# Attention loop of a hybrid encoder: one stretch of attention work per step instead of three breaks in the projections

## The reference, cut to what matters

```python
proj = h @ w_in                       # (1024, 1024) x (1024, 10240), in fp32
qkv = proj[..., :N_DIL * 3 * A_WIDTH].reshape(bsz, s, N_DIL, 3, A_HEADS, A_HEAD_DIM)
for g, (window, dil) in enumerate(DILATION_PAIRS):      # three groups
    o, l = _dilated_group(qkv[:, :, g, 0], qkv[:, :, g, 1], qkv[:, :, g, 2], window, dil, slopes)
# in a group: scores = q.k/8 + alibi; p = exp(scores - m); o = p @ v / z; lse = m + log(z)
wts = softmax(stack(lses))            # merges the three groups per head
y = (merged * silu(gate)) @ w_out
```

## Time and profile before

| | us |
|---|---|
| median of three runs | 2309.37 |
| the profiled execution | 2316.02 |
| its span, first to last instruction | 2314.2 |
| TensorE busy | 2149.2 (93%) |
| VectorE / ScalarE / GpSimd busy | 1085.6 / 939.5 / 829.3 |
| mean granted clock of TensorE | 0.977 of full speed |

### The profile page before, as it was taken

The page is one execution under the profiler, slowest core; times in us unless marked ns, Lnnn a source line. Parts: engine busy times, 40 slices in busy tenths (PEclk is TensorE's granted clock), DMA queues, the critical chain, the costliest instruction groups (busy, mean ns, idle before and its releaser), DMA issues. The chain is left out here.

```text
span 2314.2 us, 32869 instructions
## 1 busy us (share of the span) xinstructions
PE 2149.2 (93%) x11583; PEld 1695.0 (73%) x11583; DVE 1085.6 (47%) x2233; ACT 939.5 (41%) x2346; POOL 829.3 (36%) x436
## 2 busy tenths in 40 slices
PE   3999999999999999999998868689999999998997
PEld 3777777777777777777776656567777777777776
DVE  5622222222223222222224666569669579567454
ACT  2233433334333343333334134276366376375320
POOL 0211141321412214123133341156467366376472
PEclk9989999999999999999999989899999999999999
DMA  8711121211212112121122331334444344356431
GB/s 332 266 33 37 38 67 37 61 33 39 65 37 67 37 39 65 37 67 37 38 56 72 103 111 37 115 113 151 128 130 151 125 151 146 105 169 194 163 130 55
DMA packets 81406, 222.11 MB, mean 96 GB/s; under 512 B 16101, under 2 KB 34661, under 8 KB 74601
## 3 DMA queue, kind: packets, MB, share of 16 engines
q1 hardware_dynamic: 81256, 219.98, 29.6%
HBM read 195.75 MB, written 24.19 MB: 95 GB/s over the span
## 5 line engine op out<-in xcount | busy, mean ns | idle before, releaser
L476 PE MATMUL pp<-h_hi,w_hi 128*128 128x512 f32 x1264 | 513.7, 406 | 0.5 <-issue 0.4
L412 POOL TENSOR_TENSOR w_lo<-w_raw,w_hi 128x1024 fp32r<-128x1024 f32 x80 | 193.0, 2413 | 888.3 <-ACT w_hi L702 888.3
L476 PE MATMUL pp<-h_lo,w_hi 128*128 128x512 f32 x1264 | 496.0, 392 | 0.0
L476 PE MATMUL pp<-h_hi,w_lo 128*128 128x512 f32 x1264 | 493.4, 390 | 0.0
L947 DVE COPY probT<-tp 128x512 f32<-128x512 f32 x160 | 103.2, 686 | 578.9 <-PE tp L509 578.9
L1692 PE MATMUL pp_s<-h_hi,w_hi_s 128*128 128x512 f32 x640 | 279.9, 437 | 29.0 <-DVE stage_s L2287 21.1
L476 PEld LDWEIGHTS pp<-h_hi,w_hi 128*128 128x128 f32 x1264 | 237.4, 188 | 90.0 <-issue 39.8
L762 ACT ACTIVATE prob<-prob,mz 128x256 f32<-128x256 f32 (+1 forms) x384 | 176.6, 462 | 281.8 <-DVE mz L928 281.8
L476 PEld LDWEIGHTS pp<-h_hi,w_lo 128*128 128x128 f32 x1264 | 237.8, 188 | 52.3
L476 PEld LDWEIGHTS pp<-h_lo,w_hi 128*128 128x128 f32 x1264 | 238.0, 188 | 43.7
L1692 PE MATMUL pp_s<-h_hi,w_lo_s 128*128 128x512 f32 x640 | 253.5, 396 | 0.0
(11 more groups left out here) (412 smaller groups left out, 3514.8 us busy)
## 6 DMA issues: line engine op xcount, KB each, us to landing
w_raw<-in_a_w SPq DMA_DIRECT2D x80, 512.0 KB, 3.4
rw<-cum_rows SPq DMA_DIRECT2D x32, 1024.0 KB, 4.8
w_raw_s<-in_b_w SPq DMA_DIRECT2D x40, 512.0 KB, 3.4
ew<-exp_rows SPq DMA_DIRECT2D x64, 256.0 KB, 4.2
trunk<-in_ada_w SPq DMA_DIRECT2D x8, 1536.0 KB, 6.8
num_wide<-merge_rows SPq DMA_DIRECT2D x16, 768.0 KB, 7.8
num_wide<-in_ada_w SPq DMA_DIRECT2D x8, 1024.0 KB, 7.7
yT_b<-trunk SPq DMA_DIRECT2D x32, 256.0 KB, 2.3
```

The lines of the kernel that those rows point to most:

```text
L412: nc.gpsimd.tensor_tensor(w_lo[:, slot].rearrange("p k c -> p (k c)"), w_raw[:, slot].rearrange("p k c -> p (k c)"), w_hi[:, slot].rearran ...
L476: last = nc.tensor.matmul(pp[:, par, :], w[:, slot, k, :], keep[h][:, k, half * HALF:(half + 1) * HALF], start=(k == 0 and n == 0), stop=( ...
```

## The change

In the seven pairs of the loop a step is now: transposes of V of the last step, if any; values of duo d - 1; scores of duo d + 1; transposes of duo d; (statistics); then all eight quarters of units 2d and 2d + 1. The last duo's values stand at the end of the pair. In front of the loop, the column products, gate products and the first scores move before unit 11, and on ScalarE the first two softmaxes before the evacuation of unit 11. The last pair keeps its order. The same instructions run; VectorE, GpSimd and SyncE keep theirs in the same order.

```diff
--- before.py
+++ after.py
@@ -605,6 +605,13 @@
                     if k == KT - 1:
                         last.then_inc(pp_full, 1)
             for un in range(2, 12):
+                if un == 11:
+                    pe.wait_ge(n_used, KT)
+                    pe.wait_ge(t_free, T0 + 2)
+                    column_products(tp[:, 0], n_acc, ncol_full)
+                    pe.wait_ge(gate_copied, 1)
+                    gate_products(1, n_acc[:, 2 * D:3 * D])
+                    scores(0, 0)
                 for part in range(4):
                     project(un, un % 2, un // 2, un // 2 % 2, un % 2, part)
                 if un == 8:
@@ -614,63 +621,76 @@
                     for half in range(2):
                         at = (0 if un == 3 else 2) + half
                         transpose_v(at, at % 2, half, (4 if un == 3 else 10))
-            pe.wait_ge(n_used, KT)
-            pe.wait_ge(t_free, T0 + 2)
-            column_products(tp[:, 0], n_acc, ncol_full)
-            pe.wait_ge(gate_copied, 1)
-            gate_products(1, n_acc[:, 2 * D:3 * D])
-            scores(0, 0)
 
             FIRST_TILE_AT = {5: (0, 1), 6: (2, 3), 7: (4, 5), 8: (6,)}
 
-            def pair(j, table, tiles, last_pair):
-
-                base_u = 20 * j + 12
-                base_t = NT * j
-
-                def proj(u, part):
-
-                    q = 4 * u + part
-                    n = q // 4
-                    if n < 2 * tiles:
-                        project(base_u + n, n % 2, 10 * j + (6 + n // 2), (n // 2) % 2, n % 2, q % 4)
+            def proj(j, tiles, u, parts):
+
+                if u < 2 * tiles:
+                    for part in parts:
+                        project(20 * j + 12 + u, u % 2, 10 * j + (6 + u // 2), u // 2 % 2, u % 2, part)
+
+            def new_v(j, d, table):
+
+                if d in V_AT and ("v", V_AT[d], 0) in table:
+                    for half in range(2):
+                        n = table[("v", V_AT[d], half)]
+                        transpose_v(NT * j + (T0 + n), n % 2, half, 20 * j + 12 + (2 * d + 2))
+
+            def new_probs(j, d, table):
+                for u in (2 * d, 2 * d + 1):
+                    n = table[("p", u)]
+                    transpose_probs(j, u, NT * j + n, n % 2)
+
+            def new_stats(j, table):
+                n = table[("s", 0)]
+                transpose_stats(NT * j + (T0 + n), n % 2)
+
+            def duo_values(j, d, table):
+                values(j, d, NT * j + table[("p", 2 * d + 1)])
+
+            def pair(j):
 
                 for d in range(DUOS):
-                    proj(2 * d, 0)
-                    proj(2 * d, 1)
-                    for u in (2 * d, 2 * d + 1):
-                        n = table[("p", u)]
-                        transpose_probs(j, u, base_t + n, n % 2)
-                    if d == 8 and last_pair:
-                        n = table[("e", 0)]
-                        transpose_early_stats(base_t + (T0 + n), n % 2)
-                    if d == 9:
-                        n = table[("s", 0)]
-                        transpose_stats(base_t + (T0 + n), n % 2)
+                    if d:
+                        new_v(j, d - 1, T_AT)
+                        duo_values(j, d - 1, T_AT)
                     if d < DUOS - 1:
                         scores(j, d + 1)
-                    elif not last_pair:
+                    new_probs(j, d, T_AT)
+                    if d == DUOS - 1:
                         scores(j + 1, 0)
-                    proj(2 * d, 2)
-                    proj(2 * d, 3)
-                    if last_pair and d in FIRST_TILE_AT:
+                        new_stats(j, T_AT)
+                    proj(j, 10, 2 * d, range(4))
+                    proj(j, 10, 2 * d + 1, range(4))
+                duo_values(j, DUOS - 1, T_AT)
+
+            def last_pair(j):
+                for d in range(DUOS):
+                    proj(j, 4, 2 * d, range(2))
+                    new_probs(j, d, T_LAST)
+                    if d == 8:
+                        n = T_LAST[("e", 0)]
+                        transpose_early_stats(NT * j + (T0 + n), n % 2)
+                    if d == 9:
+                        new_stats(j, T_LAST)
+                    else:
+                        scores(j, d + 1)
+                    proj(j, 4, 2 * d, range(2, 4))
+                    if d in FIRST_TILE_AT:
                         if d == 5:
                             pe.wait_ge(pp_free, 20 * PAIRS + 2)
                             pe.wait_ge(y_lo_done, 1)
                         tile_0 = out_products(0, FIRST_TILE_AT[d])
                         if d == 8:
                             tile_0.then_inc(part_done, 1)
-                    values(j, d, base_t + table[("p", 2 * d + 1)])
-                    for part in range(4):
-                        proj(2 * d + 1, part)
-                    if d in V_AT and ("v", V_AT[d], 0) in table:
-                        for half in range(2):
-                            n = table[("v", V_AT[d], half)]
-                            transpose_v(base_t + (T0 + n), n % 2, half, base_u + (2 * d + 2))
+                    duo_values(j, d, T_LAST)
+                    proj(j, 4, 2 * d + 1, range(4))
+                    new_v(j, d, T_LAST)
 
             with pe.Fori(0, PAIRS - 1) as j:
-                pair(j, T_AT, 10, False)
-            pair(PAIRS - 1, T_LAST, 4, True)
+                pair(j)
+            last_pair(PAIRS - 1)
             most, all_ = range(PAIRS - 1), range(PAIRS)
             for m in range(1, 4):
 
@@ -815,9 +835,9 @@
                 if un % 2 == 0 and un >= 2:
                     n = un // 2 + 1
                     split_hi(n, n % 2, n // 2 + 1)
-            evacuate(0, 11, 1, K1, 1, 0)
             softmax(0, 0)
             softmax(0, 1)
+            evacuate(0, 11, 1, K1, 1, 0)
 
             def weights_at(j, f):
                 split_hi(10 * j + (6 + f), f % 2, 5 * j + (3 + f // 2 + 1))
```

## The result

The change makes the kernel slightly slower: 2320.06 us (median of 16 runs, 2314.75 to 2324.78) against 2311.36 (16 runs, 2305.17 to 2318.83), a ratio of 1.0037 with the interval [1.0028, 1.0047], or +8.7 us. I had forecast -3.2. The time lies inside the range and within the 0.5% that one small measurement can tell, but the interval excludes both zero and a gain.

The account below looks back on a forecast made before the run. The loop was taken to be as long as TensorE's program. Terms -19.2 (loop), +8.0 (passage), +0.2 (last pair's entry) and +7.8 (back edge) summed to -3.2 us, applied to the median 2309.4: 2306 us, range 2293 to 2322.

Parts of the forecast that it names:

- loop, seven pairs: Attention loop: 70 steps each 0.19 us cheaper, plus 2.7 and 3.2 us, saves 19.2 us; bounds 4 to 28.
- passage: Before the loop: TensorE idles 4.4 us, then column products and unit 11 meet a low clock; costs 8.0 us, bounds 4.4 and 9.
- back edge: Loop's branch: values in front cover the instruction fetch less; 1.3 us six times, 7.8 us cost, bounds 0 and 15.6.
- a lead of over 5 us: At the loop's branch: the sequencer runs about 24 projections or more ahead of TensorE, which hides the fetch.
- case of N = 24: At the loop's branch: a sequencer lead of 24 matmuls would lose 2.6 us; fewer were held excluded.
- rival D: Clock falls inside the loop, at each pair's tenth step; seven low spells cost 45 us, 2351 us; chance 0.05.
- The statistics: Their transpose in each pair no longer waits for VectorE's copy, covered by scores: 0.45 us saved seven times, 3.2 us.
- V's transposes: Three steps of each pair: no longer splitting a run of projections, they save 0.13 us, 21 times, 2.7 us.
- one mode change less a step: Loop step: three tiling-mode changes instead of four; by that rule alone 0.1 us a step, 7 us in all.
- ScalarE's 1.8 us of cover: At a pair's second step: slack before TensorE needs ScalarE's evacuation; cost nothing, at most 2 us per pair if gone.
- C: In the loop's steps: new seams cost 0.11 us for each of two, loop saves only 4; 2321 us; chance 0.12.
- B: Seams hidden: back edge stays as it was, passage clock falls no earlier; -14.6 us, 2295 us; chance 0.25.

Follow-up runs that it names:

- e10: The kernel before with TensorE's loop over seven pairs written out, nothing else: 2313.33 us, ratio 1.0016.
- e1: The changed kernel with TensorE's loop over seven pairs written out, so no branch is taken: 2295.24 us, ratio 0.9934 to the kernel before.
- e4: The kernel before with duo 9's values moved behind unit 19, directly in front of the branch, in the loop's seven pairs: 2330.41 us, ratio 1.009.
- e9: The changed kernel with only the scores before unit 11, products behind it, VectorE's first maxima before the columns, and TensorE's loop written out: 2287.29 us, ratio 0.9893.
- e2: The changed kernel with duo 9's values one unit forward, 24 projection matmuls between them and the branch: 2292.09 us, ratio 0.9914 to the kernel before.
- e8: The changed kernel with only scores before unit 11, products behind, VectorE's first maxima before the columns, and duo 9's values one unit before the branch: 2288.75 us, ratio 0.9901.
- e7: The changed kernel with 18 projection matmuls between duo 9's values and the branch: 2295.78 us in one execution, used only for its trace.
- e3: The changed kernel with the old passage: products and first scores behind unit 11, ScalarE's evacuation before the softmaxes: 2314.24 us, ratio 1.0012 to the kernel before.
- e5: The changed kernel with 6 projection matmuls between duo 9's values and the branch: 2297.73 us in one execution, used only for its trace.

## Why the prediction was wrong

The sum by its own terms, measured in the traces of the first part:

| term | forecast | measured | from |
|---|---|---|---|
| loop, seven pairs | -19.2 | -25.6 | 7 x (146.80 - 143.15), e10 and e1 |
| passage | +8.0 | +8.4 | 28.5 - 20.1 |
| last pair's entry | +0.2 | not measured | too small to be read |
| back edge | +7.8 | +25.9 | 27.15 - the 1.3 of before |
| sum | -3.2 | +8.7 | first part +8.8, medians +8.7 |

The close agreement of the sums is in part luck: from the last pair of the loop to the second layer, executions of like code differ by 2 us (212.7 in e10, 210.6 in e4).

**The step that failed is the loop's back edge**, in two places.

1. *The lead was read off the wrong packet.* I took the instruction packet at 715.9 us for the branch's own and concluded a lead of over 5 us, " excludes fewer than 24". But between branches packets of instructions come every 19 to 25 us anyway, and that one, 20 us behind the last, belongs to this cadence. The branch's packet is the next: at each branch of every kernel that keeps the loop one starts 0.7 to 4.5 us behind a regular one, and in the written-out loops of e1, e9 and e10 none does. In the kernel before it is under way between 719 and 719.5 us (queue, kind, packets, MB, share):

```profile
q8 instruction: 1, 0.02, 10.9%
```

The boundary, 721.41, comes 2.3 us behind its start. In the changed kernel the values end at 285.34, and the packet is under way between 285.34 and 285.7:

```profile
q8 instruction: 1, 0.02, 25.7%
```

TensorE resumes at 288.46, some 3 us behind the packet. In e2 the packet starts at 281.8, the boundary is at 284.83. So the sequencer asks for its target page 2.5 to 3 us before it can go on; in the kernel before, the projections queued cover all but 0.3 of that at this branch, and the 1.02 us of values cover almost none. The formula's own case of N = 24 was 2.6 us; measured are 2.5 to 3.05. The forecast took the middle of its bounds, 1.3, with no row to favour it. For the idling alone the bound of 15.6 did hold: 16.4, less the 1.3 of before, is 15.1. "Runtime: NRT & Kernel Launch" of the Trainium skill (Instruction fetch mechanics) says that a taken branch whose target is outside the pages held must fetch it before execution goes on: the trace agrees, at this price. "TensorE: Matmul & The Clock Gate" of the Trainium skill (the opening table) gives a queue of 64 entries, by which I had N = 32; the trace disagrees, unless something else ends the lead earlier: in e2 the packet starts 3.0 us before the boundary, the time of 13 projections.

2. *The clock was not priced.* Of the 27.15 us by which the six periods are longer, 16.4 is idling, and some 10.8 is work at half the clock behind five of the stops. This term, put at nothing without a reason, made the kernel slower: without it the sum would be -2.1, no change that can be told. I had rival D for a falling clock, but looked for it in the tenth step, a dense stretch. It doesn't occur there (e1: 1.00 over 1058 us). In the earlier trace rows the fall in the passage followed one-column products; I didn't ask what an idle at a branch would do, though my own passage term assumed that idling lowers the clock.

**What was right.** That TensorE's program is the loop's length, and that row-to-row starts price a step. The stretch saves the forecast's upper bound, 0.32 a step, where 0.19 was taken: 22.1 us for 70 steps against 13.3. What I had mis-sized is the transposes, 1.02 instead of 0.85: the earlier trace rows shows them in front of scores, and here projections follow. The statistics saved what was said (0.45 a pair, 3.1 us in all). V's transposes did not: they cost 0.79 and 0.10 for the second entry before, and 0.86 to 0.87 now (the first two steps with them last 14.88 and 14.89, those without 14.00 to 14.06, in e1), so 0.02 was saved each time instead of 0.13, 0.4 us instead of 2.7. By "TensorEngine Tiling (Array Packing)" of the Trainium skill (Key Properties) I had one mode change less a step. The count agrees, the 0.1 us a change that I gave it does not: 0.32 was measured, and 0.26 in e2 for one change more. Whether it is the change of mode or the re-entry into the projections that costs this, no run tells apart. ScalarE's 1.8 us of cover were enough, no wait for it came in the loop.

**The rivals.** C (the seams eat the gain) gave the right time, 2321, by luck: its step of 14.4 is refuted by 14.03. B's free back edge is refuted, its cheap step is not. D is refuted in its place. My list of what to look for named "one to two microseconds" at six branches; six there were, of 2.5 to 3.05.

The two ends of the loop, the passage (priced at 8.0, in part by luck) and the back edge (a third of it priced), then gave back more than the loop gained: 8.4 + 25.9 against 25.6. Taken away, in e8 and e9, the same stretch is worth about 1%.

## What to carry to other kernels

Before you put short instructions in front of a hardware branch, ask how many microseconds of queued work they leave: here 16 short matmuls hid nothing and 24 long ones all, and moving one group by a unit turned 8.7 us lost into 17.9 won. Tell a branch's own instruction packet from the regular ones by their cadence before you build a bound on it. And price a stop of a few microseconds twice, once for itself and once for the clock behind it.

## What the runs showed of the hardware

- Behind a taken branch on TensorE the next row comes 2.5 to 3.0 us after the start of the branch's own instruction packet, 3.5 to 3.8 where a regular packet started 0.7 to 0.9 us ahead (e7). Behind long projections this hides but for 0 to 0.2 us of idling; behind 16 short matmuls 2.5 to 3.3 us of "issue" show (changed kernel, e3, e4), none where the loop is written out (e1).
- The granted clock fell to 0.50 at thirteen of eighteen stops of 2.5 to 3.3 us (changed kernel, e3, e4), and at none of the six of 1.0 to 1.4 us in e5. A fall at such a stop costs 1.5 to 3.1 us more.
- Eight 128x128 transposes cost, by starts, 0.79 us between projections, 0.96 from projections to scores or values, 0.85 from scores to projections and 1.02 from values to scores. So 0.17 hangs on what follows and 0.06 on what stands in front; the printed durations (1.03 to 1.09) don't show it.
- The second layer, untouched, took 941.7 to 950.0 us over the twelve profiled executions. An effect of under ten microseconds had to be read where it was made, not in the total.
